# Latent attention in turns, scores, values: two banks of turned tiles, and the next head's projections in the banks of the scores

## What is computed

```
q = (rmsnorm(c_q, g_q) @ w_uq).reshape(bsz, seq, B_HEADS, QK_NOPE_DIM + QK_ROPE_DIM)
kv = (rmsnorm(c_kv, g_kv) @ w_ukv).reshape(bsz, seq, B_HEADS, QK_NOPE_DIM + V_HEAD_DIM)
q_pe = rope(q_pe, cos, sin);  k_pe = rope(k_pe, cos, sin)
s = (qn @ k_nope.T + qp @ k_pe.T) * (QK_NOPE_DIM + QK_ROPE_DIM) ** -0.5
s = where(key_idx <= q_idx, s, finfo(float32).min)
o = softmax(s) @ v
return (o * silu(z)) @ w_out_b
```

## Time and profile before

| | |
|---|---|
| median of 3 runs | 2726.3 us |
| lowest and highest | 2725.35 and 2726.92 us |
| the profiled execution's own time | 2725.38 us |
| its span in the profile | 2723.6 us |
| instructions | 51955 |
| TensorE busy (matmuls) | 2651.4 us, 97% |
| VectorE busy | 1187.9 us, 44% |
| ScalarE busy | 654.5 us, 24% |
| GpSimd busy | 1164.5 us, 43% |
| data moved | 152.72 MB |

### The profile page before, as it was taken

The page is one execution under the profiler, slowest core; times in us unless marked ns, Lnnn a source line. Parts: engine busy times, 40 slices in busy tenths (PEclk is TensorE's granted clock), DMA queues, the critical chain, the costliest instruction groups (busy, mean ns, idle before and its releaser), DMA issues.

```text
span 2723.6 us, 51955 instructions
## 1 busy us (share of the span) xinstructions
PE 2651.4 (97%) x21824; PEld 2075.9 (76%) x21824; DVE 1187.9 (44%) x1244; ACT 654.5 (24%) x914; POOL 1164.5 (43%) x1451
## 2 busy tenths in 40 slices
PE   8999999999999999999999989999999999999999
PEld 6677778888888888888888766666677777777787
DVE  7744421223522122212256664443555555544874
ACT  4433310010211000000123334443231223111331
POOL 7633335455655455545585631113313222322550
PEclk9999999999999999999999999999999999999999
DMA  3110001112111111111122200001111111113441
GB/s 133 40 32 32 32 32 47 48 51 110 47 46 46 54 46 46 54 46 46 46 79 84 85 32 16 15 16 56 41 34 45 43 39 45 40 49 118 155 155 62
DMA packets 41084, 152.72 MB, mean 56 GB/s; under 512 B 5600, under 2 KB 6112, under 8 KB 39008
## 3 DMA queue, kind: packets, MB, share of 16 engines
q1 hardware_dynamic: 30240, 106.01, 11.7%
q10 hardware_dynamic: 10688, 44.31, 4.3%
HBM read 129.34 MB, written 20.97 MB: 55 GB/s over the span
## 4 chain that ended last, share of the span: by engine, by line
PE 89%; DVE 5%; ACT 2%; DMA 1%; issue 1%; ACTq 0%; POOL 0%; POOLq 0%; DVEq 0%; SPq 0%
PE dps L300 54%; PE dps L318 14%; PE aps L1732 6%; PE aps L1356 3%; PE aps L2524 2%; PE dps L654 1%; PE dps L1369 1%; PE dps L645 1%; PE aps L632 1%; PE dps L1377 1%; ACT mla_pt L1492 1%; PE aps L1634 1%; PE aps L1893 1%; DVE h_lo L363 1%; PE dps L2524 1%
## 5 line engine op out<-in xcount | busy, mean ns | idle before, releaser
L2707 POOL TENSOR_TENSOR w_hi<-w_raw,one 128x256 fp32r<-128x256 f32 x718 | 489.0, 712 | 1468.7 <-PE dps L300 996.1
L2712 POOL TENSOR_TENSOR w_lo<-w_raw,w_hi 128x256 fp32r<-128x256 f32 x718 | 654.5, 941 | 0.5
L300 PE MATMUL dps<-h_hi,w_hi 128*128 128x512 f32 x1600 | 503.4, 393 | 14.8 <-POOL w_lo L2712 10.8
L300 PE MATMUL dps<-h_hi,w_lo 128*128 128x512 f32 x1600 | 499.2, 390 | 0.0
L300 PE MATMUL dps<-h_lo,w_hi 128*128 128x512 f32 x1600 | 499.2, 390 | 0.0
L300 PEld LDWEIGHTS dps<-h_hi,w_hi 128*128 128x128 f32 x1600 | 300.2, 188 | 83.5 <-POOL w_lo L2712 10.8
L300 PEld LDWEIGHTS dps<-h_hi,w_lo 128*128 128x128 f32 x1600 | 301.1, 188 | 63.1
L300 PEld LDWEIGHTS dps<-h_lo,w_hi 128*128 128x128 f32 x1600 | 301.2, 188 | 62.6
L318 PE MATMUL dps<-h_hi,w_hi 128*128 128x512 f32 x528 | 181.3, 414 | 5.3 <-ACT rw_b L2190 2.5
L318 PE MATMUL dps<-h_lo,w_hi 128*128 128x512 f32 x528 | 177.8, 406 | 2.1 <-ACT rw_lt L2239 1.5
L318 PE MATMUL dps<-h_hi,w_lo 128*128 128x512 f32 x528 | 175.0, 408 | 1.0 <-DVE rw_akt L2102 0.8
(11 more groups left out here) (474 smaller groups left out, 3975.2 us busy)
## 6 DMA issues: line engine op xcount, KB each, us to landing
w_raw<-w_stream SPq DMA_DIRECT2D x192, 512.0 KB, 3.4
gates<-gate_out ACTq DMA_DIRECT2D x16, 512.0 KB, 2.6
gate_ring<-gates ACTq DMA_DIRECT2D x14, 512.0 KB, 4.7
x_again<-x_t ACTq DMA_DIRECT2D x1, 4096.0 KB, 12.6
x_t<-x_res ACTq DMA_DIRECT2D x4, 1024.0 KB, 4.1
x_again<-x_t ACTq DMA_DIRECT2D x4, 1024.0 KB, 7.4
out_t<-row_x SPq DMA_DIRECT2D x16, 256.0 KB, 2.1
back<-branches ACTq DMA_DIRECT2D x7, 512.0 KB, 8.0
```

The lines of the kernel that those rows point to most:

```text
L300: mm = k.nc.tensor.matmul(k.dps[0:rows, pair, h * HALF:(h + 1) * HALF], w[:, slot, sub + t, 0:rows], x(t)[:, h * HALF:(h + 1) * HALF], sta ...
L2707: g.tensor_tensor(k.w_hi[:, s, at], k.w_raw[:, s, at], ones, ALU.mult).then_inc(k.sem("w_hi_done"), 1)
L2712: return g.tensor_tensor(k.w_lo[:, s, at], k.w_raw[:, s, at], k.w_hi[:, s, at].bitcast(F32), ALU.subtract)
```

## The change

It moves work on TensorE inside a head and gives two uses of PSUM other banks.

1. `mla_turned(k, g)`: even groups are turned into `dps[:, 1, 0:HALF]` as before, odd ones into `dps[:, 0, 0:HALF]`. A turn waits for the copy two groups back.
2. In step s TensorE first turns all groups of block s-2, then makes the scores of block s (or the next projections), then the values of all groups of block s-2. Values are no longer a group behind.
3. The projections go to the banks of the scores: the queries to the first two banks of `aps`, keys and values to the last two. They wait for the exponentials that read these banks. The keys don't wait for the drain of the queries. The first projections wait for `latent_std_done`. The next head's scores wait for the drained values, by a semaphore `mla_kv_done`.
4. Of the uses of `dps[:, 0]` only the gate product is left to count (`MLA_USES` 5 to 1), and TensorE waits for its drain before the first group that is turned there.
5. `mla_k` keeps its two halves as before: each head's 64 nope rows are drained into one, the rotary rows stand in the other for all heads.

```diff
-MLA_USES = 5
+MLA_USES = 1
+def mla_turned(k, g):
+    return k.dps[:, 1 - g % 2, 0:HALF]
 def mla_pe(k, pe):
+    pe.wait_ge(k.sem("latent_std_done"), 2)
     mla_queries_pe(k, pe, 0, 0)
     mla_keys_pe(k, pe, 0, 0)
+def mla_sums(k, part):
+    return k.aps[:, 2 * part:2 * part + 2, :]
+def mla_product_pe(k, pe, i, sub, n_k, part, x_hi, x_lo, done):
+    pe.wait_ge(k.sem("w_split"), mla_block(i) + 2)
+    for t in range(n_k):
+        for n, (w, x) in enumerate(((k.w_hi, x_hi), (k.w_hi, x_lo), (k.w_lo, x_hi))):
+            for h in range(2):
+                mm = k.nc.tensor.matmul(mla_sums(k, part)[:, h, :], w[:, 1, sub + t, :], x[:, t, h * HALF:(h + 1) * HALF],
+                                        start=t == 0 and n == 0, stop=t == n_k - 1 and n == 2)
+    mm.then_inc(k.sem(done), 1)
@@ turn(g)
-            if g:
-                pe.wait_ge(k.sem("mla_pt_done"), c)
+            if g >= 2:
+                pe.wait_ge(k.sem("mla_pt_done"), c - 1)
@@ mla_pair_pe, a head
-        pe.wait_ge(k.sem("pair0_out"), mla_use(i, h) + 3)
-        pe.wait_ge(k.sem("mla_q_done"), i * 2 + (h + 1))
+        pe.wait_ge(k.sem("mla_kv_done"), i * 2 + (h + 1))
         scores(0)
...
-        g = 0
+        if h == 0 or not end:
+            pe.wait_ge(k.sem("pair0_out"), (i + h) * MLA_USES + (MLA_USE0 + 2))
         for s in range(2, KT + 2):
+            groups = [g for g in range(N_GROUPS) if GROUPS[g][0] == s - 2]
+            for g in groups:
+                turn(g)
             if s < KT:
                 scores(s)
-            elif s == KT:
-                ahead(mla_queries_pe)
             else:
-                ahead(mla_keys_pe)
-            while g < N_GROUPS and GROUPS[g][0] == s - 2:
-                turn(g)
-                if g:
-                    values(g - 1)
-                g += 1
-        values(N_GROUPS - 1)
+                pe.wait_ge(k.sem("mla_exp_done"), i * 16 + (8 * h + s - 1))
+                ahead(mla_queries_pe if s == KT else mla_keys_pe)
+            for g in groups:
+                values(g)
@@ mla_proj_dve
-    v.tensor_tensor(k.mla_q[:, :], k.dps[:, 0, :], k.inv_q[:, :], ALU.mult).then_inc(k.sem("pair0_out"), 1)
+    v.tensor_tensor(k.mla_q[:, :], mla_sums(k, 0).rearrange("p a b -> p (a b)"), k.inv_q[:, :], ALU.mult).then_inc(k.sem("mla_q_done"), 1)
...
-    v.tensor_tensor(k.mla_vt[HD:P, :], k.dps[HD:P, 0, :], k.inv_kv[HD:P, :], ALU.mult).then_inc(k.sem("pair0_out"), 1)
+    v.tensor_tensor(k.mla_vt[HD:P, :], kv[HD:P, :], k.inv_kv[HD:P, :], ALU.mult).then_inc(k.sem("mla_kv_done"), 1)
```

More of the change, by code:

```diff
@@ L1319, in mla_block @@
     return i * 2 + (BLK["mla"] + 5)
-def mla_use(i, h):
-    return i * MLA_USES + (MLA_USE0 + 1 + 2 * h)
 def mla_gate_pe(k, pe, i):
@@ L1338, in mla_queries_pe @@
         pe.wait_ge(k.sem("latent_lo_done"), 3)
-    dense(k, pe, mla_block(i), 1, 3 * h, rows(k.cq_hi), rows(k.cq_lo), 2, 0, mla_use(i, h), "mla_proj_done")
+    mla_product_pe(k, pe, i, 3 * h, 2, 0, k.cq_hi, k.cq_lo, "mla_proj_done")
 def mla_keys_pe(k, pe, i, h):
-    dense(k, pe, mla_block(i), 1, 3 * h + 2, rows(k.ckv_hi), rows(k.ckv_lo), 1, 0, mla_use(i, h) + 1, "blk_done" if h else "mla_proj_done")
+    mla_product_pe(k, pe, i, 3 * h + 2, 1, 1, k.ckv_hi, k.ckv_lo, "blk_done" if h else "mla_proj_done")
 def mla_pair_pe(k, pe, i, end):
@@ L1365, in turn @@
             pe.wait_ge(k.sem("mla_exp_done"), i * 16 + (8 * h + b + 1))
-            if g:
-                pe.wait_ge(k.sem("mla_pt_done"), c)
+            if g >= 2:
+                pe.wait_ge(k.sem("mla_pt_done"), c - 1)
             for t in range(n):
-                mm = k.nc.tensor.transpose(k.dps[:, 1, t * P:(t + 1) * P], k.mla_p[:, b % 2, (first + t) * P:(first + t + 1) * P], ident)
+                mm = k.nc.tensor.transpose(mla_turned(k, g)[:, t * P:(t + 1) * P], k.mla_p[:, b % 2, (first + t) * P:(first + t + 1) * P], ident)
             mm.then_inc(k.sem("mla_t_done"), 1)
@@ L1434, in mla_proj_dve @@
     v = k.nc.vector
-    use = mla_use(i, h)
     dve.wait_ge(k.sem("mla_proj_done"), i * 3 + (2 * h + 1))
-    v.tensor_tensor(k.mla_q[:, :], k.dps[:, 0, :], k.inv_q[:, :], ALU.mult).then_inc(k.sem("pair0_out"), 1)
-    dve.wait_ge(k.sem("pair0_out"), use + 2)
-    v.tensor_tensor(k.mla_q[HD:P, :], k.mla_q[HD:P, :], k.trig[HD:P, :], ALU.mult).then_inc(k.sem("mla_q_done"), 1)
+    v.tensor_tensor(k.mla_q[:, :], mla_sums(k, 0).rearrange("p a b -> p (a b)"), k.inv_q[:, :], ALU.mult).then_inc(k.sem("mla_q_done"), 1)
+    dve.wait_ge(k.sem("mla_q_done"), i * 2 + (h + 1))
+    v.tensor_tensor(k.mla_q[HD:P, :], k.mla_q[HD:P, :], k.trig[HD:P, :], ALU.mult)
     if h:
@@ L1443, in mla_proj_dve @@
         dve.wait_ge(k.sem("mla_proj_done"), i * 3 + 2)
-    v.tensor_tensor(k.mla_k[0:HD, :], k.dps[0:HD, 0, :], k.inv_kv[0:HD, :], ALU.mult).then_inc(k.sem("mla_k_done"), 1)
-    v.tensor_tensor(k.mla_vt[HD:P, :], k.dps[HD:P, 0, :], k.inv_kv[HD:P, :], ALU.mult).then_inc(k.sem("pair0_out"), 1)
+    kv = mla_sums(k, 1).rearrange("p a b -> p (a b)")
+    v.tensor_tensor(k.mla_k[0:HD, :], kv[0:HD, :], k.inv_kv[0:HD, :], ALU.mult)
+    v.tensor_tensor(k.mla_vt[HD:P, :], kv[HD:P, :], k.inv_kv[HD:P, :], ALU.mult).then_inc(k.sem("mla_kv_done"), 1)
 def mla_pair_dve(k, dve, i, end):
@@ L1491, in mla_act @@
                     w = GROUPS[g][2] * P
-                    a.activation(k.mla_pt[:, g % 2, 0:w], k.dps[:, 1, 0:w], ACT.Copy).then_inc(k.sem("mla_pt_done"), 1)
+                    a.activation(k.mla_pt[:, g % 2, 0:w], mla_turned(k, g)[:, 0:w], ACT.Copy).then_inc(k.sem("mla_pt_done"), 1)
                     g += 1
```

## The result

The changed kernel takes 2713.4 us (median of 5 runs, 2710.9 to 2714.2), the kernel before 2726.3. The profiled execution took 2712.65 us (span 2710.8).

What follows compares the result with a forecast made beforehand. TensorE, busy 97% of the span, was taken to bound the kernel. The terms summed to -5.6 us at full clock and +0.6 for the clock, so -5.0: 2721 us against a median of 2726.3, range 2716.5 to 2727.5.

Steps and rivals of the forecast that it cites:

- Waits (a): TensorE's waits for the copy mla_pt, due to the single bank of turned tiles, would go: -10.1 us.
- Passages (b): Weight loads stand on "issue" when TensorE passes from turns to values; four fewer passages a head: -4.5 us.
- Turns ahead of the scores: Turning before the scores fills a little of TensorE's wait for the softmax: 0.14 us a head, 1.1 gained in all.
- the new wait of the values: Values right behind their turns wait for ScalarE's copy in the short steps: 0.6 us a head, 5.0 lost in eight.
- The last head: No next projections cover ScalarE at steps 8 and 9 there: 1.8 us more.
- Start: At the start the keys are done before VectorE asks, so mla_k's idle 0.55 us goes: 0.5 gained.
- the middle of the last pair: Without a gate product, TensorE waits 1.4 us for mla_vt plus some 0.5 for the softmax, instead of 2.33: 0.5 gained.
- Pair ends: Less work behind the keys covers the drains up to mla_o: TensorE idles 2.2 us, not 0.8; 4.3 lost at three.
- The clock: One of four idles is followed by half clock, as one was before, and the first idle lengthens: net +0.6 us.
- the wait moves to ScalarE: Rival: the values wait 1.3 us a head for ScalarE's copy, or passages do not get fewer: 2726 us; chance 0.21.
- The pair ends go cold: Rival: half clock after the idle for mla_o at three pair ends, 2.8 us each: 2731 to 2739 us; chance 0.10.
- Warm throughout: Rival: the middle of the last pair stays at full clock and no pair end goes cold: 2718.5 us; chance 0.22.

Runs made afterwards that it cites:

- experiment 1: The change with the loop order of the kernel before, two banks of turned tiles and the moved projections kept: 2716.6 us, ratio 0.9969.
- experiment 5: The change with the values of a block's second group put between the next block's two groups of turns, three times a head: 2721.6 us, ratio 0.9983.
- experiment 4: The change with VectorE draining mla_o before mla_vt at the end of the first three pairs: 2708.3 us, ratio 0.9935.
- experiment 6: The change plus 14 turns of the identity ahead of TensorE's wait for mla_o at three pair ends: 2707.8 us, ratio 0.9934.

## Why the prediction was wrong

The direction held, and the size was short by 7.6 us. The new order inside a head was booked at -4.5 - 1.1 + 5.0 + 1.8, a loss of 1.2 us, and the runs show a gain of about 8.7. Its steps in turn:

- **Waits (a), -10.1.** Right: -9.2 by the heads of experiment 1, -9.0 by its median, with the spread told there.
- **Passages (b), -4.5. This step failed.** The prediction read the price of a group that stands apart from the "issue" rows, 0.17 us less 0.03, and called it a passage from turns to values. Experiment 5 shows 0.30 us by its heads: two fixed parts, 0.14 of the turns and 0.15 of the values. The count was off by a little the other way. A head before passed from turns to values 11 times, not 12, because its last two groups of values stand together; the weight loads of the values have 88 stops in rows 3, 80 on "issue" and 8 on mla_pt, which is 11 in each of eight heads. So the new order saves 32 runs of turns and 24 runs of values: 32 x 0.14 + 24 x 0.15 = 8.1 us. The upper bound, 5.4, was read off one kind of row and was no bound. The Trainium skill (TensorE: Matmul & The Clock Gate, Step-by-step: what each phase is for) has weight loads pulled ahead of running matmuls, and by it the term would have been nil; experiment 5's rows of 1.74 and 1.45 us for the same work speak against using it so.
- **Turns ahead of the scores, -1.1, and the new wait of the values, +5.0. This is the other step that failed.** The new wait costs the matmuls 3.7 us in all and 1.9 of that is in the last head, 1.55 and 0.34 in a row. In the others some 0.2 to 0.3 us each stand at step 3, not the walk's 0.6 over four steps. Below are steps 3 and 4 of a head in the change. What the turns ahead of the scores save was booked too low beside it: the warm second heads of experiment 1 and of the change differ by 26.05 - 24.76 = 1.29 us without their waits for mla_o. Four runs of turns and three of values fewer are 1.0 of it, so both effects together are -0.3 a head, where +0.5 was booked. Without the new wait of 0.26 us the turns' place gives some 0.5 a head, 4.3 in eight. This is what is left over; no run tests it by itself.
- **The last head, +1.8.** Right as a wait, 1.9; it is part of the 3.7.
- **Start, -0.5, and the middle of the last pair, -0.5.** In the middle the wait for mla_vt is 1.4 us as forecast (7.1 in two, less 5.7) and the softmax behind it is awaited 0.44, where 2.33 stood before. The start can't be told apart from the first head; its cold stretch grew from 3.4 to 6.8 us.
- **Pair ends, +4.3.** 2.51 for 0.80 us, +5.1 in three. The chain of drains was right; the 32 value records ahead of it take 1.15 us, not 1.44. Experiment 4 takes back 4.1.
- **The clock, +0.6.** One of four idles was to go cold. Two pair ends did, and the last head, cold before, stayed warm. The two cold ends cost 1.8 and 1.6 us, +3.4. The last head gave back 2.8, by the prediction's own pair of rows: no wait stands inside either, and another warm head of the kernel before takes 4.56 us for them as well. So the net is +0.6, the number that was booked, by more cold ends than booked at a lower price each; that is luck.

Why a cold stretch is cheaper at a pair end than in the last head shows in the waits there. The first pair's end stayed warm, and TensorE waits 0.53 and 0.74 us for VectorE and ScalarE behind it; behind the second, cold end these waits are 0.27 and 0.16, and behind the third there are none. A part of the slower work stands where TensorE would have waited. First the warm end, then the cold one:

```profile
1684.32 0.70 PE L1372 MATMUL aps<-mla_k,mla_q 128*128 128x256 f32 x2 [0.53 <-DVE mla_out L1488]
...
1685.82 0.33 PE L1385 MATMUL dps<-const,mla_p 128*128 128x128 f32 x1 [0.74 <-ACT mla_p L1512]
```

```profile
1749.59 1.22 PE L1372 MATMUL aps<-mla_k,mla_q 128*128 128x256 f32 x2 [0.27 <-DVE mla_out L1488]
...
1751.08 0.48 PE L1385 MATMUL dps<-const,mla_p 128*128 128x128 f32 x1 [0.16 <-ACT mla_p L1512]
```

The rule of the Trainium skill (TensorE: Matmul & The Clock Gate, A second HAM failure mode: psum-queue depth-cycling) that short idles make the clock swing is borne out here at two pair ends of three, and experiment 6 shows that the idle is what did it. It did not decide the sign, because even three such ends at 1.7 us would cost some 5 us.

Steps 3 and 4 of a head in the change, for the walk of the new wait (all engines; L1375 the mask of scores 3, L1506 the copy of three tiles):

```profile
1688.18 0.22 PE L1375 MATMUL aps<-mla_mask_r,ident_r 128*128 128x128 bf16 x1
1688.66 0.45 PE L1393 MATMUL dps<-mla_v,mla_pt 128*64 128x64 f32 x8 [0.26 <-ACT mla_pt L1506]
...
1690.03 0.48 ACT L1506 ACTIVATE mla_pt<-dps 128x384 f32<-128x384 f32 x1
...
1690.66 0.57 PE L1393 MATMUL dps<-mla_v,mla_pt 128*64 128x64 f32 x12
```

The copy is ready at 1690.51 (1690.03 + 0.48), 2.33 us after the start of the mask of scores 3, where the walk had 2.5. TensorE needs 2.48 us, 0.26 of it the wait of step 3 and 2.22 its own pieces, where the walk had 2.1. So step 3's wait spares step 4 all of its own. The walk had named this ("what one step waits is spared the next") and then added steps 2 to 5 up all the same.

With these in place the sum is -9.2 - 8.1 - 4.3 + 3.7 - 0.5 - 0.5 + 5.1 + 0.6 = -13.2 us, against -12.9 measured. Its -4.3 is a remainder taken from two heads, so the agreement supports the other terms only to about 1 us, which is also the size by which the medians of equal kernels here differ (2725.6 to 2726.3).

Of the rivals, "the wait moves to ScalarE" is refuted: the matmuls see 3.7 us. "The pair ends go cold" was half true: two of three did, at 1.7 us each where 2.8 was booked. "Warm throughout" is what experiment 6 makes of the change: 2707.8, where 2718.5 was given. Of the signs that were to show each step, "no wait of turns for mla_pt" and the pair ends were right; "some 64 passages of 0.17 us" was wrong, since the weight loads of the values now stand on mla_pt (48 times, 21.6 us), behind scores that cover it. The stage is 13.0 us shorter by the table, where 5 were forecast. By the prediction's own words more than one cold pair end would make it wrong, and it did, but on the side that cost time; the gain came from the row that it had called settled.

## What to carry to other kernels

When an order joins short groups of matmuls, take the price of a group from start-to-start times of groups of different length (the part that doesn't shrink with the length), not from the idle rows of the weight loads: here 0.14 us for the turns and 0.15 for the values, 0.30 together where the idle row says 0.17. A second bank and an order that needs it should be tried together: the bank alone gave 9.0 us, the order alone cost 49.2, both gave 12.9. And when work moves ahead of an engine's wait, look at what the other engine has queued before the thing waited for: changing the place of one drain gave 4 to 5 us more.

## What the runs showed of the hardware

- A run of products has a fixed part of 0.14 to 0.15 us when TensorE passes between 128 x 128 turns and 128 x 64 values, with all operands ready and no wait in the rows (experiment 5: 1.74 us apart, 1.45 together).
- A stretch of 6.8 us at clock 0.50 cost 1.8 and 1.6 us at the pair ends, where TensorE's waits shrank from 1.27 us to 0.43 and to none, and 2.8 us in the last head of the kernel before, in rows without a wait. In experiment 1 that head's cold stretch is half as long, and the same rows take 6.06 us, where they took 7.33 cold and 4.56 warm:

```profile
1845.28 1.19 PE L1372 MATMUL aps<-mla_k,mla_q 128*128 128x384 f32 x2 [2.33 <-ACT mla_p L1514]
...
1851.34 1.56 PE L1372 MATMUL aps<-mla_k,mla_q 128*128 128x512 f32 x4
```

- The length of an idle alone did not tell what the clock would do. Idles of 2.51 us were followed by 1.00 at one pair end of the change and by 0.50 at two; in experiment 5 by 0.50 at all three; in experiment 4 idles of 1.15 us by 0.50 at one end of three.
- Turns of the identity in the idle time, 1.75 us in a wait of 2.5, kept the clock at 1.00 afterwards at both ends where it had fallen to 0.50.
- The value products' wait shows as 21.6 us on the weight loads and 3.7 us on the matmuls. The walk of steps 3 and 4 goes by the second.
